# Linear attention: gates amid alternating query and key tiles, paired state updates; products behind layer norms; first scores amid value tiles

## The chip, the cores and the metric

The kernel runs on one core of one Trainium2 chip. The time is device microseconds of that core. The kernel before took 1971.51 us (median of three runs, 1969.75 to 1971.76). A change of under about 0.2% (3.9 us) can't be told from none.

## The reference, cut to what matters

Two blocks for 512 tokens of width 1024, all in float32. The first: a hybrid mixer, cross attention and a gated convolution layer. The second has two layers, each followed by a layer norm after its mixer and one after its MLP, so four in all:

```python
for i in range(2):
    mix = nsa_pool_mixer(x, ...) if i % 2 == 0 else gla_mixer(x, ...)
    x = layer_norm(ALPHA * x + mix, ln1_g[i], ln1_b[i])
    x = layer_norm(ALPHA * x + sqrelu_mlp(x, ...), ln2_g[i], ln2_b[i])
```

The NSA mixer is attention over compressed, selected and window keys for 8 query heads in 2 groups, beside a pooling path. The linear-attention mixer (GLA) has 4 heads with keys of 128 and values of 256 features. It projects x to queries, keys, values, a gate of rank 16 and an output gate r. The log gates are a log-sigmoid of the rank-16 gate times a second weight; they are summed within each chunk of 64 tokens. Per chunk the output is the masked local scores times the values, plus the query times the state left by the chunks before it; the state decays and takes in the chunk's keys times values. The output is normed and multiplied by silu(r).

## The kernel before, in words

Activations lie in SBUF with features on the partitions (8 chunks of 128) and 512 tokens along the free axis. A weight matrix is a stream of tiles of 128 x 1024 floats: SyncE loads each into one of four slots, GpSimd splits it into a high and a low part in fp32r (L2334 and L2336), and TensorE makes three fp32r products of 128x512 per chunk (high by high, high by low, low by high), 24 for a whole tile. A tile ends with `tile_done`; GpSimd may refill its slot then. VectorE or ScalarE takes the result out of the PSUM bank and counts `tile_out`; `claim` (in `dense`) makes TensorE wait for the `tile_out` of four tiles before. Each engine follows an order written out by hand, and waits on semaphores hold up all that is queued behind them.

**Layer norms.** `residual_ln` on VectorE adds each of the 8 result tiles into h (`take`, L1736), and keeps a running sum over chunks (L1698, for the last one L1700). TensorE turns it into the mean in all partitions by a product with ones (`sum_features`, L563), and the squares likewise (`sum_squares`, L556). Mean and squares give the variance (VectorE L1709), ScalarE the inverse root (L1164, L1165), and then, per chunk, VectorE scales (L1718), ScalarE writes the high part (L1237) and VectorE the low part (L1725). The next stage begins with `opening_of`: three tiles at once, chunk by chunk, six products for the high part of a chunk (L493, L494), three for its low part (L497).

**NSA.** Two tiles give the values by tokens (`tokens`, products of 128x256, L518 to L520) after the last key tile. Then come the scores of the first batch (`n_scores(0)`, L895 and L899), turns of the compressed probabilities (L942), the scores of batch 1, which reuse the banks of the values and so wait for them to be taken out (ScalarE L1475), and a pipeline over 16 batches: maximum on VectorE (L2153), exponentials on ScalarE (`n_exp`, L1462), scaling, turns and value products.

**GLA.** Nine tiles (gate, four of queries, four of keys), then four products of 16x512 for the gates' second weight (L1021), then two groups of four value tiles (`tokens`, 128x512, L518 to L520). ScalarE takes out all queries and keys and then works through the gates head by head in turns with VectorE: bias, Abs, Exp, Ln (L1531 to L1534), scan on VectorE (L2236, L2237), two exponentials, three products on VectorE (L2239, L2240, L2242), an exponential (L1541), a product (L2246, counts `gla_k`). The value tiles are taken out after heads 1 and 3 (L1160). `gla_scores` (L1048, turns L1052) waits for all four heads. Then eight tiles of r (`r_tile`, L1033 to L1035); among the chunks of the first four lie seven state updates each (`gla_updates`, L1066), one after each chunk from the second on. VectorE makes the states (L2266, L2269), and the next update but one waits for a state because the updates alternate between two banks. `gla_out` makes, for each block of 128 tokens, a local product (L1084) and one or two state products (L1088).

Of the kernel before, what the change touches and what calls it, by code (L numbers as in the profile page):

```python
# [25 lines left out]
S = 512  # L26
MEM = 256
KC = D // P
# [90 lines left out]
def chunk(c):  # L119
    return slice(c * P, (c + 1) * P)  # L120


def weight_stream(i):
# [5 lines left out]
    def add(w, cols, k0=0, kc=KC):  # L129
        tiles.append(tile_of(w, k0, kc, cols))  # L130
# [54 lines left out]

    mlp(0)
    add(c_in, slice(3072, 3088))
    for c in range(8):
        add(c_in, chunk(c))
    for half in range(2):  # L190
        add_wide(c_in[:, D + half * 512:D + (half + 1) * 512], 512)
    for c in range(KC):
# [259 lines left out]
def tensor_program(pr, pe):  # L452
# [45 lines left out]
                if k == kc - 1:  # L498
                    last.then_inc(sem("tile_done"), 1)

    def tokens(t0, width, hi, lo, blocks):

        per = TILE // width
        tiles = KC // per
        for j in range(tiles):
            pe.wait_ge(sem("weights_split"), t0 + j + 1)
            w_hi, w_lo = (m[w][:, (t0 + j) % RING].rearrange("p k n -> p (k n)") for w in ("w_hi", "w_lo"))
            for b in range(blocks):  # L510
                per_bank = 512 // width
                first, final = b % per_bank == 0, b % per_bank == per_bank - 1
                if j == 0 and first:
                    pe.wait_ge(sem("tile_out"), t0 + b // per_bank - RING + 1)
                out = acc[:, (t0 + b // per_bank) % RING, blk(b % per_bank, width)]
                for i in range(per):
                    k = j * per + i
                    mm(out, hi[:, k, blk(b)], w_hi[:, blk(i, width)], start=k == 0 and first, stop=False)  # L518
                    mm(out, hi[:, k, blk(b)], w_lo[:, blk(i, width)], start=False, stop=False)  # L519
                    last = mm(out, lo[:, k, blk(b)], w_hi[:, blk(i, width)], start=False,  # L520
                              stop=k == KC - 1 and final)
            last.then_inc(sem("tile_done"), 1)

    def late_opening(t0, first_tile, norm):

# [32 lines left out]
    def sum_features(name, part):  # L558


        i = LAYER_NORMS.index(name)
        pe.wait_ge(sem("ln_sum"), 2 * i + part + 1)
        mm(misc[:, 0, :], ones, m["sum_h"], start=True, stop=True).then_inc(sem("ln_mean"), 1)  # L563


    pe.wait_ge(sem("const_in"), 16)
    def idle_products(n):

        for _ in range(n):
            mm(acc[:, 0], ones, m["const"][:, 0:S], start=True, stop=True)  # L570

    idle_products(2)
    sum_squares("mix")
# [308 lines left out]

    pe.wait_ge(sem("cmp_gap"), 2)
    pool_out(0)
    tokens(t0 + 13, 256, x_hi, x_lo, TB)

    def n_scores(b):

# [44 lines left out]
                          start=False, stop=b == last_of(tb) and sb == tb)  # L933
        last.then_inc(sem("n_values"), 1)

    pe.wait_ge(sem("tile_out"), t0 + 13)
    n_scores(0)
    pe.wait_ge(sem("n_const"), 1)
    for half in range(2):
        pe.wait_ge(sem("cmp_p"), half + 1)  # L940
# [43 lines left out]
    def normed_stage(name, norm):  # L984

        for c in range(3, KC):
            if c == HALF + 1:
                sum_features(norm, 0)
            dense(START[name] + c, (START[name] + c) % RING, y_hi, y_lo)
        sum_features(norm, 1)  # L990
        sum_squares(norm)

    def mlp_group(name, g, norm, high, next_norm=None):
        t0 = g * 16 + START[name]
        opening(t0, START[name], norm)
        for j in range(3, 8):
            dense(t0 + j, (START[name] + j) % RING, x_hi, x_lo)
        opening_of(t0 + 8, START[name] + 8, y_hi, y_lo, high, "tile_out", g * 8, ready_before=t0)
        for c in range(3, KC):
            if next_norm and c == HALF + 1:  # L1000
                sum_features(next_norm, 0)
            dense(t0 + 8 + c, (START[name] + 8 + c) % RING, y_hi, y_lo)
        if next_norm:
            sum_features(next_norm, 1)
            sum_squares(next_norm)

    def mlp(name, norm, high, next_norm):
        with pe.Fori(0, GROUPS - 1) as g:
# [5 lines left out]
    mlp("mlp_a", "ln1a", "mlp_a_high", "ln2a")  # L1014


    stage("gla_in", x_hi, x_lo, 9, norm="ln2a")
    gate_w2 = pr.view("gate_w2").rearrange("p (h n) -> p h n", h=4)
    pe.wait_ge(sem("tile_out"), START["gla_in"] + 1)
    for head in range(4):  # L1020
        mm(misc[:, head, :], gate_w2[0:16, head], m["a_g"][0:16], start=True, stop=True).then_inc(sem("gla_z"), 1)  # L1021
    for part in range(2):
        tokens(START["gla_in"] + 9 + 4 * part, 512, x_hi, x_lo, TB)

    def r_tile(c, beside=None):

# [28 lines left out]
    def gla_updates(head):  # L1055

        def beside(k):
            if k == 0:
                return
            n = k - 1  # L1060
            i = 7 * head + n
            if n == 0:
                pe.wait_ge(sem("gla_kd"), head + 1)
            if i >= 2:
                pe.wait_ge(sem("gla_state"), i - 1)
            mm(misc[:, 1 + i % 2, 0:256], m["kd_tok"][blk(n % 2, 64), head % 2, n // 2],  # L1066
               m["v_g"][blk(n % 2, 64), n // 2, blk(head, 256)], start=True, stop=True).then_inc(sem("gla_update"), 1)
        return beside

    def o_bank(head, tb):  # L1070
# [4 lines left out]
    def gla_out(head):  # L1075
# [29 lines left out]
    def feature_beside(head, e, step):  # L1105
# [40 lines left out]
def scalar_program(pr, act):  # L1146
# [322 lines left out]
            .then_inc(sem("n_y_high"), 1)  # L1469

    pool_high(0)
    act.wait_ge(sem("tile_out"), t0 + 13)
    act.wait_ge(sem("tile_done"), t0 + 15)
    for tb in range(TB):
# [7 lines left out]
    n_exp(0)  # L1482
    n_exp(1)
    pool_high(1)
    for b in range(len(BATCHES)):
# [33 lines left out]

    t0 = START["gla_in"]  # L1520
    out(t0, t0 % RING, m["a_g"][0:16], src=acc[0:16, t0 % RING])
    for c in range(4):
        out(t0 + 1 + c, (t0 + 1 + c) % RING, m["q_g"][:, c])
    for c in range(4):
        out(t0 + 5 + c, (t0 + 5 + c) % RING, m["k_g"][:, c])
    gz, gt, gb = m["gz"], m["gt"], m["gb"]
    for head in range(4):
        act.wait_ge(sem("gla_z"), head + 1)
        if head:
            act.wait_ge(sem("gla_k"), head)  # L1530
# [1 line left out]
        own.link(f(gt, gz, ACT.Abs))  # L1532
        own.link(f(gt, gt, ACT.Exp, scale=-1.0))
        f(gt, gt, ACT.Ln, bias=1.0).then_inc(sem("gla_ln"), 1)  # L1534
        act.wait_ge(sem("gla_b"), head + 1)
        f(gz, gb, ACT.Exp, scale=1.0 / 16).then_inc(sem("gla_exp"), 1)
        f(gt, gb, ACT.Exp, scale=-1.0 / 16).then_inc(sem("gla_exp"), 1)
# [4 lines left out]
        if head % 2:  # L1542
            t = t0 + 9 + 4 * (head // 2)
            for b in range(TB):
                out_wide(t + b, t + 3, m["v_g"][:, b, blk(head // 2, 512)])
    def gla_kd(head):
        act.wait_ge(sem("gla_turned"), head + 1)
        if head >= 2:
# [48 lines left out]
def vector_program(pr, dve):  # L1597
# [74 lines left out]
    def residual_ln(name, t0, add):  # L1672
# [751 lines left out]
```

## Time and profile before

| | us |
|---|---|
| median of the runs | 1971.51 |
| profiled execution, its own time | 1971.24 |
| its span, first to last instruction | 1969.4 |
| TensorE busy | 1897.1 (96%) |
| GpSimd busy | 1069.4 (54%) |
| VectorE busy | 791.0 (40%) |
| ScalarE busy | 432.1 (22%) |
| mean granted TensorE clock | 0.987 of full |

The profile's page gives busy times and the chain of work that ended last. TensorE's idle time is what the rest of the span consists of, and it lies in few places; the timeline of one engine in a window shows each piece, with the engine and line that ended it in brackets. A product that shows 0.39 us starts 0.23 us after the one before it: the records overlap, so costs are read from start to start. The products of a 32-bit operand that isn't fp32r have two records each (x2 is one product).

### The profile page before, as it was taken

The page shows a single profiled execution, that of the slowest core. Times are in us where ns is not written, and L with a number is a line of the kernel's source. Part 1 is how long each engine was busy: PE and PEld are TensorE (multiplying, and loading weights), DVE is VectorE, ACT ScalarE, POOL GpSimd, SP SyncE. Part 2 cuts the span into 40 slices and gives each one's busy share as a digit, 9 for nine tenths or more (in the row PEclk, how much of TensorE's full clock was granted, in tenths as well). Part 3 has the DMA queues.
Part 4 walks back from the last instruction along what each step waited for, and adds up shares of the span by engine and source line. Part 5 has one row for each costly group of instructions (what it writes and reads, how often), then busy time and mean ns, then how long its engine had stood idle before and what let it go on. Part 6 is the DMA issues. An engine that isn't in the chain of part 4 may idle for free.

```text
span 1969.4 us, 24294 instructions
## 1 busy us (share of the span) xinstructions
PE 1897.1 (96%) x8906; PEld 1517.2 (77%) x8906; DVE 791.0 (40%) x1309; ACT 432.1 (22%) x850; POOL 1069.4 (54%) x622
## 2 busy tenths in 40 slices
PE   7989999999999999999999999998999989999996
PEld 5868787888888888866778888887765768888885
DVE  4965333352432435678451212135243372112126
ACT  4323422310000121155140101113323141101022
POOL 4735662566758666410546556664642446666652
PEclk9989999999999999999999999999999999999999
DMA  5322331232323335210223223332321223333321
GB/s 217 107 65 75 98 106 54 86 97 96 108 86 117 97 96 199 67 37 1 75 80 101 87 85 96 104 100 74 97 65 33 65 70 102 107 99 103 96 86 43
DMA packets 46880, 175.99 MB, mean 89 GB/s; under 512 B 5201, under 2 KB 5329, under 8 KB 46033
## 3 DMA queue, kind: packets, MB, share of 16 engines
q1 hardware_dynamic: 46512, 169.55, 27.1%
q10 hardware_dynamic: 288, 5.31, 0.7%
q8 instruction: 59, 0.97, 0.2%
q14 instruction: 21, 0.16, 0.0%
HBM read 172.74 MB, written 2.10 MB: 89 GB/s over the span
## 4 chain that ended last, share of the span: by engine, by line
PE 93%; DVE 4%; ACT 2%; issue 1%; DMA 0%; SPq 0%; DVEq 0%; ACTq 0%
PE acc L470 17%; PE acc L472 17%; PE acc L471 17%; PE acc L493 7%; PE acc L494 7%; PE acc L497 7%; PE acc L1033 1%; PE misc L1066 1%; PE acc L518 1%; PE misc L911 1%; PE acc L519 1%; PE acc L520 1%; PE acc L1035 1%; PE acc L1034 1%; PE acc L534 1%; PE acc L535 1%
## 5 line engine op out<-in xcount | busy, mean ns | idle before, releaser
L2334 POOL TENSOR_SCALAR w_hi<-raw 128x1024 fp32r<-128x1024 f32 x309 | 330.0, 1068 | 842.2 <-PE acc L497 329.5
L2336 POOL TENSOR_TENSOR w_lo<-raw,w_hi 128x1024 fp32r<-128x1024 f32 x309 | 744.1, 2408 | 25.8
L470 PE MATMUL acc<-x_hi,w_hi 128*128 128x512 f32 x872 | 342.8, 393 | 0.0
L472 PE MATMUL acc<-x_hi,w_lo 128*128 128x512 f32 x872 | 339.6, 389 | 0.0
L471 PE MATMUL acc<-x_lo,w_hi 128*128 128x512 f32 x872 | 339.3, 389 | 0.0
L470 PE MATMUL acc<-y_hi,w_hi 128*128 128x512 f32 x590 | 231.1, 392 | 0.0
L1736 DVE TENSOR_TENSOR h<-acc,h 128x512 f32<-128x512 f32 x120 | 82.9, 691 | 367.4 <-PE acc L472 233.8
L472 PE MATMUL acc<-y_hi,w_lo 128*128 128x512 f32 x590 | 229.6, 389 | 0.0
L471 PE MATMUL acc<-y_lo,w_hi 128*128 128x512 f32 x590 | 229.6, 389 | 0.0
L472 PEld LDWEIGHTS acc<-x_hi,w_lo 128*128 128x128 f32 x872 | 163.7, 188 | 34.4
L471 PEld LDWEIGHTS acc<-x_lo,w_hi 128*128 128x128 f32 x872 | 163.9, 188 | 32.5
L470 PEld LDWEIGHTS acc<-x_hi,w_hi 128*128 128x128 f32 x872 | 163.8, 188 | 32.4
L1508 ACT ACTIVATE z<-acc 128x512 f32<-128x512 f32 x64 | 38.2, 597 | 466.1 <-PE acc L497 354.9
L493 PE MATMUL acc<-y_hi,w_hi 128*128 128x512 f32 x330 | 130.0, 394 | 4.2 <-ACT y_hi L1368 2.9
L2211 DVE TENSOR_TENSOR acc<-acc,z 128x512 f32<-128x512 f32 x64 | 44.6, 697 | 216.1 <-ACT z L1508 216.1
L471 PEld LDWEIGHTS acc<-y_lo,w_hi 128*128 128x128 f32 x590 | 110.8, 188 | 23.9 <-issue 1.0
L494 PE MATMUL acc<-y_hi,w_lo 128*128 128x512 f32 x330 | 129.1, 391 | 0.0
L470 PEld LDWEIGHTS acc<-y_hi,w_hi 128*128 128x128 f32 x590 | 110.7, 188 | 23.9 <-issue 1.0
L472 PEld LDWEIGHTS acc<-y_hi,w_lo 128*128 128x128 f32 x590 | 110.7, 188 | 23.1
L493 PE MATMUL acc<-x_hi,w_hi 128*128 128x512 f32 x240 | 97.1, 404 | 15.3 <-ACT x_hi L1237 12.2
L494 PE MATMUL acc<-x_hi,w_lo 128*128 128x512 f32 x240 | 96.5, 402 | 0.0
L497 PE MATMUL acc<-y_lo,w_hi 128*128 128x512 f32 x330 | 93.1, 390 | 1.4 <-DVE y_lo L2317 1.4
(387 smaller groups left out, 2648.2 us busy)
## 6 DMA issues: line engine op xcount, KB each, us to landing
raw<-weights_dram SPq DMA_DIRECT2D x309, 512.0 KB, 3.6
w_cmp<-w_cmp_dram ACTq DMA_DIRECT2D x1, 4096.0 KB, 14.6
h<-x_dram SPq DMA_DIRECT2D x2, 1024.0 KB, 6.4
out_dram<-h SPq DMA_DIRECT2D x8, 256.0 KB, 2.0
small<-small_dram SPq DMA_DIRECT2D x1, 1408.0 KB, 16.0
small<-small_dram ACTq DMA_DIRECT2D x1, 1088.0 KB, 5.0
mem_in<-mem_dram SPq DMA_DIRECT2D x1, 1024.0 KB, 13.2
const<-const_dram SPq DMA_DIRECT2D x1, 640.0 KB, 9.3
```

The costliest lines, as they stand in the source:

```text
L470: mm(out, m["w_hi"][:, slot, k], hi[:, k], start=k == 0, stop=False)
L471: mm(out, m["w_hi"][:, slot, k], lo[:, k], start=False, stop=False)
L472: last = mm(out, m["w_lo"][:, slot, k], hi[:, k], start=False, stop=k == kc - 1)
L493: mm(acc[:, slot], m["w_hi"][:, slot, k], hi[:, k], start=k == 0, stop=False)
L494: mm(acc[:, slot], m["w_lo"][:, slot, k], hi[:, k], start=False, stop=False)
L497: last = mm(acc[:, slot], m["w_hi"][:, slot, k], lo[:, k], start=False, stop=k == kc - 1)
L518: mm(out, hi[:, k, blk(b)], w_hi[:, blk(i, width)], start=k == 0 and first, stop=False)
L1508: f(z[:, slot], acc[:, slot], ACT.Relu).then_inc(sem(name + "_relu"), 1)
L1736: v.tensor_tensor(h[:, c], acc[:, slot], h[:, c], ALU.add).then_inc(sem("tile_out"), 1)
L2211: v.tensor_tensor(acc[:, slot], acc[:, slot], z[:, slot], ALU.mult).then_inc(sem(name + "_product"), 1)
L2334: nc.gpsimd.tensor_scalar(hi, m["raw"][:, slot], 1.0, 0.0, ALU.mult, ALU.add).then_inc(sem("weights_high"), 1)
L2336: nc.gpsimd.tensor_tensor(m["w_lo"][:, slot].rearrange("p k n -> p (k n)"), m["raw"][:, slot], bf(hi), ALU.subtract).then_inc(sem("weights ...
```

## The change

- The stream alternates the query and key tiles of GLA. After the gate, query 0, key 0 and query 1 tiles come four times one gate product (L1021) and one whole tile, then the last key tile. ScalarE takes tiles out between the heads' gates; `gla_gate` is the part up to Ln, `gla_exps` the rest.
- The value tiles count a semaphore `gla_v` after each block of the last tile, so that the first three banks are taken out (`v_out`) before the tile ends. `gla_scores(0)` moves from behind the second group of value tiles to between the two groups.
- State updates come in pairs: 0 and 1 after the second chunk, 2 and 3 after the fourth, 4 and 5 after the sixth, 6 after the eighth.
- `gla_out` makes its four local products first and the state products after them.
- The second mean of a layer norm is two products that accumulate: the sum without the last chunk, then the last chunk itself once its tile is out. VectorE's last addition goes. After the sum of squares TensorE makes four products of ones (128x512, 32-bit), whose result isn't used, into the bank of the next stage's first tile; not after the last layer norm.
- `n_scores(0)` moves between the two value tiles of NSA, and `n_exp(0)` on ScalarE ahead of the values' taking out.

```diff
-    for c in range(8):
+    for c in range(4):
         add(c_in, chunk(c))
+        add(c_in, chunk(4 + c))
@@ tokens
+                if ready and j == tiles - 1 and b < blocks - 1:
+                    last.then_inc(sem(ready), 1)
             last.then_inc(sem("tile_done"), 1)
+            if beside:
+                beside(j)
@@ sum_features, part 1 (part 0 as before)
+        mm(misc[:, 0, :], ones, m["sum_h"], start=True, stop=False)
+        first = N_TILES if name == LAYER_NORMS[-1] else START[BEFORE_STAGE[name]]
+        pe.wait_ge(sem("tile_out"), first)
+        mm(misc[:, 0, :], ones, m["h"][:, KC - 1], start=False, stop=True).then_inc(sem("ln_mean"), 1)
+        sum_squares(name)
+        if first < N_TILES:
+            idle_products(4, first % RING)
@@ NSA, TensorE
-    tokens(t0 + 13, 256, x_hi, x_lo, TB)
...
-    pe.wait_ge(sem("tile_out"), t0 + 13)
-    n_scores(0)
+    def first_scores(j):
+        if j == 0:
+            pe.wait_ge(sem("tile_out"), t0 + 13)
+            n_scores(0)
+
+    tokens(t0 + 13, 256, x_hi, x_lo, TB, beside=first_scores)
@@ GLA, TensorE
-    stage("gla_in", x_hi, x_lo, 9, norm="ln2a")
+    stage("gla_in", x_hi, x_lo, 4, norm="ln2a")
...
     for head in range(4):
         mm(misc[:, head, :], gate_w2[0:16, head], m["a_g"][0:16], start=True, stop=True).then_inc(sem("gla_z"), 1)
-    for part in range(2):
-        tokens(START["gla_in"] + 9 + 4 * part, 512, x_hi, x_lo, TB)
+        t = START["gla_in"] + 4 + head
+        dense(t, t % RING, x_hi, x_lo)
+    dense(START["gla_in"] + 8, START["gla_in"] % RING, x_hi, x_lo)
@@ gla_updates
-            if k == 0:
+            if k % 2 == 0:
                 return
...
+            for n in range(k - 1, min(k + 1, 7)):
+                i = 7 * head + n
+                if i >= 2:
+                    pe.wait_ge(sem("gla_state"), i - 1)
+                mm(...)
@@ gla_out
         for tb in range(TB):
+            mm(o_bank(head, tb), m["att_g"][:, head % 2, tb], m["v_g"][:, tb, blk(head, 256)], start=tb % 2 == 0, stop=False)
+        for tb in range(TB):
             out = o_bank(head, tb)
-            mm(out, m["att_g"][:, head % 2, tb], m["v_g"][:, tb, blk(head, 256)], start=tb % 2 == 0, stop=False)
@@ GLA, TensorE
+    tokens(START["gla_in"] + 9, 512, x_hi, x_lo, TB, "gla_v")
     gla_scores(0)
+    tokens(START["gla_in"] + 13, 512, x_hi, x_lo, TB, "gla_v")
@@ GLA, ScalarE
+    q_out(0); k_out(0); q_out(1)
+    gla_gate(0); gla_exps(0); k_out(1); q_out(2)
+    gla_gate(1); gla_exps(1); k_out(2); q_out(3)
+    gla_gate(2); k_out(3); gla_exps(2)
+    gla_gate(3); gla_exps(3)
+    v_out(0)
...
     gla_kd(0)
+    v_out(1)
     r_out(0)
@@ residual_ln, VectorE
-            if k < KC - 1:
+            if k < KC - 2:
                 own.link(v.tensor_tensor(part, part, h[:, k], ALU.add))
-            else:
+            elif k < KC - 1:
                 v.tensor_tensor(total, part, h[:, k], ALU.add).then_inc(sem("ln_sum"), 1)
```

(The ScalarE calls stand one to a line in the kernel; `n_exp(0)` moves in the same way from behind the values' taking out to ahead of it.)

## Rows read from the trace of the kernel before

**Rows 1.** The page, chain of work that ended last, shares by engine.

```profile
PE 93%; DVE 4%; ACT 2%; issue 1%; DMA 0%; SPq 0%; DVEq 0%; ACTq 0%
```

**Rows 2.** Timeline, TensorE, third of four layer-norm ends: start us, us, what.

```profile
1340.42 1.12 PE L563 MATMUL misc<-sum_h,const 128*128 128x512 f32 x2 [1.58 <-DVE sum_h L1700]
1341.38 1.02 PE L556 MATMUL misc<-sum_sq,const 128*128 128x512 f32 x2
1346.45 0.77 PE L493 MATMUL acc<-x_hi,w_hi 128*128 128x512 f32 x1 [4.05 <-ACT x_hi L1237]
...
1349.97 0.40 PE L493 MATMUL acc<-x_hi,w_hi 128*128 128x512 f32 x1
```

**Rows 3.** Timelines of VectorE and ScalarE, the same stretch.

```profile
1338.94 0.69 DVE L1736 TENSOR_TENSOR h<-acc,h 128x512 f32<-128x512 f32 x1 [2.04 <-PE acc L472]
...
1340.33 0.69 DVE L1619 TENSOR_TENSOR sum_sq<-misc,sq 128x512 f32<-128x512 f32 x1
1342.44 0.70 DVE L1709 SCALAR_TENSOR_TENSOR misc<-misc,sq 128x512 f32<-128x512 f32 x1 [1.41 <-PE misc L556]
...
1347.35 0.74 DVE L1725 SCALAR_TENSOR_TENSOR x_lo<-misc,par,x_hi 128x512 fp32r<-128x512 f32 x1
...
1345.62 0.69 ACT L1237 ACTIVATE x_hi<-misc,par 128x512 fp32r<-128x512 f32 x1 [1.25 <-DVE misc L1718]
```

**Rows 4.** Timeline, TensorE, products of ones at the kernel's start.

```profile
15.81 1.88 PE L570 MATMUL acc<-const 128*128 128x512 f32 x4
```

**Rows 5.** Windows: us, busy us (x) of each engine; PEclk is the granted clock.

```profile
1346.40:1350.00 3.60, 3.55 (x10) 2.87 (x11) 3.60 (x7) 2.04 (x3) 0.00 (x0) 0.58 0.00 0
1400.00:1404.00 4.00, 4.00 (x10) 2.71 (x9) 1.92 (x2) 1.95 (x5) 0.74 (x1) 0.58 0.36 131
```

**Rows 6.** Timeline, TensorE, gate products, second group of value tiles, first scores.

```profile
1398.81 1.88 PE L1021 MATMUL misc<-a_g,small 16*128 16x512 f32 x4
...
1425.04 0.47 PE L518 MATMUL acc<-w_hi,x_hi 128*128 128x512 f32 x1 [0.78 <-ACT v_g L1160]
...
1449.45 0.69 PE L1048 MATMUL misc<-q_g,kt_g 128*64 128x64 f32 x16 [2.37 <-DVE k_g L2246]
```

**Rows 7.** Timelines of ScalarE, VectorE, GpSimd in the gates.

```profile
1398.15 0.69 ACT L1531 ACTIVATE gz<-misc,par 128x512 f32<-128x512 f32 x1 [0.46 <-PE misc L1021]
...
1407.53 0.69 ACT L1531 ACTIVATE gz<-misc,par 128x512 f32<-128x512 f32 x1 [0.82 <-DVE k_g L2246]
...
1432.14 2.92 DVE L2239 TENSOR_TENSOR kt_g<-k_g,gt 128x512 f32<-128x512 f32 x1 [1.22 <-ACT gt L1537]
...
1432.11 2.39 POOL L2336 TENSOR_TENSOR w_lo<-raw,w_hi 128x1024 fp32r<-128x1024 f32 x1
```

**Rows 8.** Timeline, TensorE, updates among r tile 0, products of head 0.

```profile
1455.06 0.70 PE L1066 MATMUL misc<-v_g,kd_tok 64*128 64x256 f32 x2
...
1456.58 0.70 PE L1066 MATMUL misc<-v_g,kd_tok 64*128 64x256 f32 x2
...
1475.32 0.70 PE L1084 MATMUL acc<-v_g,att_g 128*128 128x256 f32 x2
1475.94 0.65 PE L1088 MATMUL acc<-state,q_g 128*64 128x256 f32 x4
```

**Rows 9.** Timeline, TensorE, scores in NSA.

```profile
848.16 1.16 PE L895 MATMUL acc<-k_br,q_n 64*128 64x128 f32 x16
...
849.72 1.04 PE L942 MATMUL misc<-const,e_c 128*128 128x128 f32 x8
...
856.91 1.13 PE L895 MATMUL acc<-k_br,q_n 64*128 64x256 f32 x8
```

**Rows 10.** Timelines of VectorE and ScalarE, the same stretch.

```profile
840.46 0.68 DVE L1745 TENSOR_TENSOR k_br<-acc,r_late 128x512 f32<-128x512 f32 x1
...
848.33 1.57 ACT L1475 ACTIVATE v_br<-acc,r_col 128x256 f32<-128x256 f32 x4 [10.88 <-PE acc L520]
...
853.93 0.40 ACT L1462 ACTIVATE p_n<-acc,n_neg 128x128 f32<-128x128 f32 x1
```

More of the change, by code:

```diff
@@ L499, in opening_of, with tokens @@
                     last.then_inc(sem("tile_done"), 1)
-    def tokens(t0, width, hi, lo, blocks):
+    def tokens(t0, width, hi, lo, blocks, ready=None, beside=None):
         per = TILE // width
@@ L562, in sum_features, with idle_products @@
         pe.wait_ge(sem("ln_sum"), 2 * i + part + 1)
-        mm(misc[:, 0, :], ones, m["sum_h"], start=True, stop=True).then_inc(sem("ln_mean"), 1)
+        if part == 0:
+            mm(misc[:, 0, :], ones, m["sum_h"], start=True, stop=True).then_inc(sem("ln_mean"), 1)
+            return
+        mm(misc[:, 0, :], ones, m["sum_h"], start=True, stop=False)
[5 more added lines that the diff above has]
+            idle_products(4, first % RING)
     pe.wait_ge(sem("const_in"), 16)
-    def idle_products(n):
+    def idle_products(n, slot=0):
         for _ in range(n):
-            mm(acc[:, 0], ones, m["const"][:, 0:S], start=True, stop=True)
+            mm(acc[:, slot], ones, m["const"][:, 0:S], start=True, stop=True)
     idle_products(2)
@@ L990, in normed_stage @@
         sum_features(norm, 1)
-        sum_squares(norm)
     def mlp_group(name, g, norm, high, next_norm=None):
@@ L1004, in mlp_group @@
             sum_features(next_norm, 1)
-            sum_squares(next_norm)
     def mlp(name, norm, high, next_norm):
@@ L1057, in beside @@
         def beside(k):
-            if k == 0:
+            if k % 2 == 0:
                 return
-            n = k - 1
-            i = 7 * head + n
-            if n == 0:
+            if k == 1:
                 pe.wait_ge(sem("gla_kd"), head + 1)
[L1064 to L1067, printed above, removed]
+            for n in range(k - 1, min(k + 1, 7)):
+                i = 7 * head + n
+                if i >= 2:
+                    pe.wait_ge(sem("gla_state"), i - 1)
+                mm(misc[:, 1 + i % 2, 0:256], m["kd_tok"][blk(n % 2, 64), head % 2, n // 2],
+                   m["v_g"][blk(n % 2, 64), n // 2, blk(head, 256)], start=True, stop=True).then_inc(sem("gla_update"), 1)
         return beside
@@ L1471, in scalar_program @@
     pool_high(0)
+    n_exp(0)
     act.wait_ge(sem("tile_out"), t0 + 13)
@@ L1481, in scalar_program @@
     f(m["pct"][:, 0:4], misc[:, 1, :].rearrange("p (j n) -> p j n", j=4), ACT.Copy).then_inc(sem("cmp_pt"), 1)
-    n_exp(0)
     n_exp(1)
@@ L1521, in scalar_program, with q_out, k_out, gla_gate @@
     out(t0, t0 % RING, m["a_g"][0:16], src=acc[0:16, t0 % RING])
[L1522 to L1525, printed above, removed]
+    def q_out(c):
+        out(t0 + 1 + 2 * c, (t0 + 1 + 2 * c) % RING, m["q_g"][:, c])
+    def k_out(c):
+        out(t0 + 2 + 2 * c, (t0 + 2 + 2 * c) % RING, m["k_g"][:, c])
     gz, gt, gb = m["gz"], m["gt"], m["gb"]
-    for head in range(4):
+    def gla_gate(head):
         act.wait_ge(sem("gla_z"), head + 1)
@@ L1534, in scalar_program, with gla_exps @@
         f(gt, gt, ACT.Ln, bias=1.0).then_inc(sem("gla_ln"), 1)
+    def gla_exps(head):
         act.wait_ge(sem("gla_b"), head + 1)
@@ L1541, in scalar_program, with v_out @@
         f(gz, gz, ACT.Exp, scale=1.0 / 16).then_inc(sem("gla_exp"), 1)
[L1542 to L1545, printed above, removed]
+    def v_out(part):
+        t = t0 + 9 + 4 * part
+        for b in range(TB):
+            if b < TB - 1:
+                act.wait_ge(sem("gla_v"), (TB - 1) * part + b + 1)
+                f(m["v_g"][:, b, blk(part, 512)], acc[:, (t + b) % RING], ACT.Copy).then_inc(sem("tile_out"), 1)
+            else:
+                out_wide(t + b, t + 3, m["v_g"][:, b, blk(part, 512)])
+    q_out(0)
+    k_out(0)
+    q_out(1)
+    gla_gate(0)
+    gla_exps(0)
+    k_out(1)
+    q_out(2)
+    gla_gate(1)
+    gla_exps(1)
+    k_out(2)
+    q_out(3)
+    gla_gate(2)
+    k_out(3)
+    gla_exps(2)
+    gla_gate(3)
+    gla_exps(3)
+    v_out(0)
     def gla_kd(head):
```

## The prediction

> **What bounds the kernel now.** I read the chain of waits first: 93% of what ended last is TensorE [rows 1]. Dense fp32r products are untouched by this change, so I went on to TensorE's timeline and looked for its gaps, for stretches at the lower clock, and for places where products of another kind cost more than their columns. The second group of value tiles is 96 products from 1425.04 to 1447.08 (the next gap's start, 1449.45 less 2.37), 0.228 us each [rows 6]; a whole tile of 24 is 5.46. Each layer norm but the last leaves TensorE idle for 1.58 and then 4.05 us [rows 2], and the products after it run at a granted clock of 0.58 [rows 5]. GLA has gaps of 0.78 and 2.37 us [rows 6], a second stretch at 0.58 [rows 5], and a state update that lengthens each chunk of an r tile from 0.68 (three products) to 1.52 [rows 8].
>
> **Layer norms (four ends, three followed by an opening).** Take the one at 1338.94; the others read alike. VectorE's addition ends at 1339.63, its sum takes until 1340.4, the mean product starts at 1340.42, the squares' product behind it at 1341.38, and L1709 at 1342.44 [rows 2, 3]. After the change the first mean product runs while VectorE adds the last chunk (its input is ready a tile earlier), and the second starts at about 1339.70 and lets go at 1340.66 (0.96 start to start [rows 2]). The squares' sum on VectorE runs from 1340.33 to 1341.02 as before [rows 3], so their product starts at 1341.09 in place of 1341.38: the chain gains 0.3, not the 0.7 of the addition removed, because the squares are late next. This holds at all four ends.
>
> The four products of ones: two took 1.88 at full clock, 0.94 each [rows 4]. Started at 1341.09 + 0.96 = 1342.05 they end at 1345.8. The opening's first operand comes at 1346.45 - 0.3 = 1346.15, so they end 0.35 before it is wanted and cost nothing. What they change is the clock. Before, the opening's first chunk took from 1346.45 to 1349.97, 3.52 us for nine products [rows 2], at 0.58 [rows 5]. The idle time before it was 4.05, and 1.58 a little earlier; now no gap there is over 0.5, so I take the full level of 2.4 GHz: six products from 1346.15 to 1347.5, then a wait for the low part (its end, 1348.09, less 0.3 = 1347.8 [rows 3]), three products to 1348.5. The second chunk starts 1.45 earlier. From there TensorE's own 2.05 per chunk is slower than the 1.9 of VectorE and ScalarE, so the gain stays. 3 x 1.45 + 0.3 = 4.6 us. If the clock falls in spite of them, 4 x 0.3 = 1.2 stays. The Trainium skill (TensorE: Matmul & The Clock Gate, Part 1) says that an idle engine falls to the lower clock and busy work lifts it again; the trace agrees, at 0.58 after the 4.05 us.
>
> **GLA: gates amid the tiles.** TensorE's work up to r tile 0 stays: 6 dense tiles after the opening, 4 gate products, 192 products of value tiles, scores and turns 1.03. What goes is: the clock after four gate products in a row of 16 rows each (0.58 from 1400 to 1404 [rows 5]: its nine products cost 3.5 for 2.05, so 1.45; a single such product between whole tiles gives no such stretch, I take it); the gap of 0.78 and its restart, 0.95, since three of four banks are now taken out while the tile runs; the gap of 2.37, 2.5 with its restart, if the gates are done in time [rows 6]. With 0.3 of pipeline ends this is 5.2. Bounds: 3.7 if the clock falls again, 5.2 above, as nothing else idles there.
>
> Are the gates in time? A head's chain takes 9.38 us without GpSimd (1398.15 to 1407.53 [rows 7]). GpSimd's split of a tile holds up VectorE products of two SBUF operands: L2239 at 1432.14 took 2.92 in place of 0.69, while L2336 ran from 1432.11 [rows 7]; a hit costs up to 2.2. I put GpSimd's splits (1.07 + 2.39, started by the tile that frees the slot) beside the new order. With all of it 1.4 earlier: gate 0 starts at 1369.3, head 0 is hit three times and ends at 1382.4; gate 1 starts at 1382.8 and ends at 1394.2; gate 2 starts at 1394.7 (behind the query tile of 1393.6), waits for the last key tile at 1399.0, ends at 1406.0; gate 3 ends at 1417.0. The scores want it at the end of the first value group: the opening's end (1349.97 + 7 x 2.04 = 1364.26, now 1362.8) + 6 x 5.45 + 4 x 0.88 + 21.85 = 1420.9. 3.9 us are spare, so the chain is hidden. The tiles held up behind it on ScalarE: key 1 leaves its bank at 1382, and the first that needs that is the last key tile at 1393.6; key 2 at 1394 against 1400.4; key 3 at 1399.7 against 1403.2. None waits. The first value bank is ready at 1416.9, when ScalarE is just free. `gla_scores(0)` needs no bank of the values. r tile 0 then starts 5.2 + 1.45 earlier.
>
> **Paired updates.** Before, an update costs 1.52 - 0.68 = 0.84, though its 256 columns in a 32-bit operand are about 0.43 by the 0.94 of 512 [rows 8, 4]: half is for going from one kind of product to the other and back. Of a pair the second goes without that: 0.43 more. And the two use different halves of the rows (64*128) and different banks; four such products of 256 in NSA (x8, two records each, alternating halves) take 1.13 in all, 0.28 each (at 856.91 [rows 9]). A pair then costs between 0.84 (second free) and 1.46 (0.84 + the 0.62 of an isolated L1084 [rows 8]); I take 1.05, nearest to the NSA row. An r tile saves 3 x (1.68 - 1.05) = 1.9, for the tiles of heads 0 to 2 5.6 us (bounds 2.0 and 7.6). The added wait: the second update of a pair wants the state of the one two before, which VectorE now makes in a run of two (0.43 to 0.48 each, done about 1.05 after the pair); the next pair comes 1.37 after it, so 0.3 is spare. In head 3 it isn't: VectorE has a gain and a scaling (0.75 and 1.65) among the states, update 3 waits about 0.4 and updates 4 and 5 another 0.6. I give that tile 0.9. Sum 6.5.
>
> The skill (TensorEngine Tiling (Array Packing), Key Properties) says that a change of tiling mode drains the engine and that different row tiles run in parallel. Both would be in the 0.84 and in the 0.28 that the rows show. By its factor of up to 2 a pair would be at the lower bound, 0.84, and the kernel 1.9 us faster than I say.
>
> **`gla_out`.** Now a block of 128 tokens costs 0.62 for the local product (1475.32 to 1475.94) and 0.59 for two state products (0.65 less the overlap with what follows) [rows 8]. In a run the local ones should cost 0.43 + 0.06 = 0.49 and a pair of state products about 0.5 (a little under the NSA row's 0.28 each). That is 3 x 0.13 + 3 x 0.09 = 0.65 per head; I take 0.6, 2.3 us for four heads; bounds 0 and 3.4 (columns alone). The first blocks now finish later, but ScalarE's two squares for them (0.7) still fit before the last block's.
>
> **NSA.** The value tiles end at 848.16 [rows 9]; the second's 48 products of half the columns take half of 0.228 and a little more each, 5.8, so the first ends at about 842.3. The last key tile's output ends at 841.14 [rows 10], so `n_scores(0)` doesn't wait. It takes 1.56 (848.16 to 849.72 [rows 9]) and pushes the end of the value tiles and the values' taking out (1.57 on ScalarE, 848.33 to 849.90 [rows 10]) by as much, to 851.45. The scores of batch 1 need that bank: they started at 850.69, behind the turns (0.97 after 849.72); now 851.5, 0.8 later. Their maximum then ends at 854.5. `n_exp(0)` is done by 848, but before, `n_exp(1)` started at 853.93 [rows 10], right behind it and 0.3 after its own maximum. So the exponentials that were the bound are replaced by the later scores: 0.6 us later, and the chain `n_exp(1)`, pool output, maximum 2, `n_exp(2)` passes it on. Cost 0.6 (bounds -1.0, if the lighter ScalarE catches up later, and 1.6, the whole scores).
>
> **Sum.** 4.6 + 5.2 + 6.5 + 2.3 - 0.6 = 18.0 us off the profiled execution's own 1971.24: 1953.2. Its span was 1.84 shorter. The median of the runs is 0.27 above that execution, so 1953.5.
>
> **Rivals.**
> A. The products of ones don't hold the clock. For it: the fall after the gate products came although TensorE was busy all through them. Against: the second pair of products of ones at the start ran at 0.94 each, the full level. LN gain 1.2 in place of 4.6: 1956.9. 10%.
> B. Pairs cost what two updates cost alone: 1.46, and the waits for states bite. For it: the rows show the two halves side by side only without waits between. The r tiles give 2.0 + 0.3 and `gla_out` 1: 1959. 17%.
> C. The gate chain isn't done by 1420.9. Two more hits by GpSimd use up the 3.9 spare; two beyond that cost 2 to 4: 1957. 10%.
> D. The other side: the gate chain becomes the bound of the whole stage. ScalarE holds query and key tiles behind it, so that value tiles stall on their banks. From 1369.3 to 1420.9 each head has 12.9 us; the chain eats the whole gain at (51.6 + 18.0)/4 = 17.4 us per head, and at 18.5 the kernel is slower by 4.4: 1976. Measured without GpSimd 9.38, worst with it 13.1. It would need every one of the five VectorE products of a head to be hit (9.38 + 5 x 2.2 = 20.4). 2%.
> E. The edits do little together (the clock in both places falls, the pairs at 1.46, no gain in `gla_out`): 18.0 - 3.4 - 1.5 - 4.3 - 2.3 = 6.5, 1965. 4%.
>
> **Chances.** The forecast 57%, A 10, B 17, C 10, D 2, E 4. Range 1949.5 (pairs at 0.84, `gla_out` at its upper bound, and NSA a little better) to 1960.5, which takes in A, B and C and leaves out E and D. About 0.2% (3.9 us) is what can be told from no change. Faster 0.95, within 0.03, slower 0.02.
>
> **What would show it.** Layer norms: the opening's first products 0.23 apart and the second chunk 1.45 earlier; L1709 0.3 earlier against L1736. GLA: no gap between gate products and value tiles, none before `gla_scores`, granted clock 1.0 throughout, and 81.0 us from the end of the opening to r tile 0 in place of 86.2 (1364.26 to 1450.48). r tiles 0 to 2: 9.4 in place of 11.3. `gla_out`: 4.1 in place of 4.7. NSA: `n_exp(1)` 0.6 later. Wrong if r tiles stay over 10.5, if VectorE's states lag behind the pairs, or if TensorE waits for `gla_k` between the value groups.

## The result, and the profile after

The changed kernel took 1950.07 us (median of 4 runs, 1948.35 to 1950.29), the kernel before 1970.97 beside it on the same chip (4 runs, 1969.75 to 1971.76). The ratio is 0.989, with a 95% interval of 0.9878 to 0.9903: about 21 us faster, where I had forecast 18.0. The profiled execution took 1950.14 us, its span was 1948.4 and the mean granted clock 0.991 of full (0.987 before). Every part of the change gained or lost in the direction that I had worked out. Three terms had the wrong size, and one had the right size for a wrong reason.

Chain of work that ended last, from the page of the changed kernel [rows 1]:

```profile
PE 94%; DVE 3%; ACT 1%; issue 1%; DMA 0%; SPq 0%; DVEq 0%; ACTq 0%
```

TensorE's timeline at the same layer-norm end as in rows 2 (it is the second of the four, not the third as they call it: TensorE's full means start at 982, 1340, 1594 and 1953 in the kernel before); L570 and L573 are the two parts of the mean, L560 the squares, L583 the products of ones:

```profile
1338.15 1.02 PE L570 MATMUL misc<-sum_h,const 128*128 128x512 f32 x2
1339.16 1.12 PE L573 MATMUL misc<-h,const 128*128 128x512 f32 x2
1340.60 1.13 PE L560 MATMUL misc<-sum_sq,const 128*128 128x512 f32 x2 [0.32 <-DVE sum_sq L1669]
1341.57 3.60 PE L583 MATMUL acc<-const 128*128 128x512 f32 x8
1345.78 0.47 PE L494 MATMUL acc<-x_hi,w_hi 128*128 128x512 f32 x1 [0.62 <-ACT x_hi L1255]
...
1347.47 0.97 PE L498 MATMUL acc<-x_lo,w_hi 128*128 128x512 f32 x3
1348.28 0.39 PE L494 MATMUL acc<-x_hi,w_hi 128*128 128x512 f32 x1
```

VectorE there [rows 3]:

```profile
1338.41 0.69 DVE L1786 TENSOR_TENSOR h<-acc,h 128x512 f32<-128x512 f32 x1 [2.12 <-PE acc L473]
1339.86 0.69 DVE L1669 TENSOR_TENSOR sum_sq<-misc,sq 128x512 f32<-128x512 f32 x1 [0.75 <-ACT sq L1190]
1341.77 0.70 DVE L1759 SCALAR_TENSOR_TENSOR misc<-misc,sq 128x512 f32<-128x512 f32 x1 [1.22 <-PE misc L560]
```

The two idle stretches of 1.58 and 4.05 us have become 0.32 and 0.62. The opening's first six products are 0.23 apart (0.31 behind the first), and the second chunk begins 2.50 after the first (3.52 before). The windows answer to [rows 5]; the third column from the right is the granted clock:

```profile
1346.00:1350.00 4.00, 3.93 (x17) 2.90 (x17) 4.00 (x8) 2.67 (x4) 0.00 (x0) 1.00 0.00 0
1369.00:1373.00 4.00, 4.00 (x18) 3.20 (x18) 1.02 (x1) 2.58 (x4) 3.92 (x4) 1.00 0.45 138
```

TensorE in GLA [rows 6]: a gate product (L1035) ahead of a key tile, then the first scores and turns between the two groups of value tiles, and r tile 0, which now starts with no gap anywhere before it:

```profile
1368.10 1.12 PE L1035 MATMUL misc<-a_g,small 16*128 16x512 f32 x2
1369.15 0.50 PE L471 MATMUL acc<-x_hi,w_hi 128*128 128x512 f32 x1
...
1422.16 0.69 PE L1063 MATMUL misc<-q_g,kt_g 128*64 128x64 f32 x16
...
1445.06 0.39 PE L1048 MATMUL acc<-x_hi,w_hi 128*128 128x512 f32 x1
```

The gate chain ended on VectorE 3.0 us before those scores [rows 7]:

```profile
1418.37 0.75 DVE L2296 TENSOR_TENSOR k_g<-k_g,gz 128x512 f32<-128x512 f32 x1 [0.70 <-ACT gz L1566]
```

r tile 0 and the products of head 0 [rows 8]; L1081 x4 is a pair of updates, L1098 the local products, L1104 the state products:

```profile
1446.51 0.70 PE L1081 MATMUL misc<-v_g,kd_tok 64*128 64x256 f32 x4
1447.14 0.50 PE L1048 MATMUL acc<-x_hi,w_hi 128*128 128x512 f32 x1
...
1448.73 0.70 PE L1081 MATMUL misc<-v_g,kd_tok 64*128 64x256 f32 x4
...
1463.65 1.99 PE L1098 MATMUL acc<-v_g,att_g 128*128 128x256 f32 x8
1465.58 1.73 PE L1104 MATMUL acc<-state,q_g 128*64 128x256 f32 x13
```

Here is the surprise of the trace. A pair has the same record as a lone update, 0.70, and the next product starts 0.63 later in both cases.

NSA, TensorE [rows 9]:

```profile
851.86 1.16 PE L907 MATMUL acc<-k_br,q_n 64*128 64x128 f32 x16 [0.84 <-ACT v_br L1494]
...
862.77 1.97 PE L923 MATMUL misc<-const,p_n 128*128 128x128 f32 x8 [3.48 <-ACT pt_n L1511]
```

Stages of one trace are compared with the same stages of the other, since the work ahead of all edits shifted by itself from execution to execution (NSA's first pool product, which no edit reaches, started between 834.1 and 837.6 in the kernels below):

| stretch | before | after | gain | forecast |
|---|---|---|---|---|
| mean product of the 1st to that of the 2nd layer norm | 358.28 | 357.16 | 1.12 | 1.45 |
| 2nd layer norm, from VectorE's last addition into h to the opening's second chunk | 11.03 | 9.87 | 1.16 | 1.45 |
| 3rd layer norm to the mean product of the 4th | 359.46 | 357.18 | 2.28 | 1.45 |
| the last layer norm's end, from the same addition to the variance | 3.50 | 3.35 | 0.15 | 0.3 |
| GLA: end of the opening to r tile 0 | 86.2 | 82.5 | 3.7 | 5.2 |
| r tiles 0 to 3 (11.3, 11.3, 11.3, 11.7 before; 8.7, 8.8, 8.8, 10.2 after) | 45.7 | 36.6 | 9.1 | 6.5 |
| products of the four heads, `gla_out` (4.74 each before) | 19.0 | 14.8 | 4.2 | 2.3 |
| NSA: first pool product to the next stage's opening | 100.13 | 100.49 | -0.36 | -0.6 |

Less 0.2 by which the work ahead of the edits was longer, that is 21.1, against 21.0 by the spans (1969.4 to 1948.4).

### The profile page after: what moved, and what is told of

It reads as the page before. It is cut to its first block, busy times and chain, and to the rows that moved or that the text cites. A ratio compares the mean times of both kernels' runs of the same rounds, so it can differ in the third digit from the quotient of the medians.

```text
span 1948.4 us, 24354 instructions
## 1 busy us (share of the span) xinstructions
PE 1894.0 (97%) x8938; PEld 1517.1 (78%) x8938; DVE 791.6 (41%) x1305; ACT 432.0 (22%) x850; POOL 1071.2 (55%) x622
## 4 chain that ended last, share of the span: by engine, by line
PE 94%; DVE 3%; ACT 1%; issue 1%; DMA 0%; SPq 0%; DVEq 0%; ACTq 0%
PE acc L471 17%; PE acc L473 17%; PE acc L472 17%; PE acc L498 7%; PE acc L494 7%; PE acc L495 7%; PE acc L518 1%; PE acc L519 1%; PE acc L520 1%; PE acc L1048 1%; PE misc L923 1%; PE acc L1050 1%; PE acc L1049 1%; PE acc L539 1%; PE acc L538 1%; PE acc L537 1%
```

## The experiments

Eleven kernels were run, all cut from the changed kernel. Where no number of runs is given the kernel ran once, and what is said of it rests on its trace, stage by stage. Line numbers in their rows can differ from its by a few.

**1. `singles`: one update per chunk again, the rest as changed.**

```
 def beside(k):
-    if k % 2 == 0:
+    if k == 0:
...
-    for n in range(k - 1, min(k + 1, 7)):
+    for n in (k - 1,):
```

> The changed kernel with the state updates one per chunk again, from the second chunk on, all else as changed. Theory (the second update of a pair is free, 0.85 us for the pair against 0.84 for one alone): r tiles of heads 0 to 2 go from 8.8 us back to 11.3, that of head 3 from 10.2 to about 11.7, and the kernel is 9 us slower than the changed one, 1959. Rival (most of the shorter r tiles comes from the better clock or the earlier gates, not from the pairs): r tiles stay under 10 us and the kernel loses under 5 us.

Measured: 1959.19 (4 runs, 1957.77 to 1959.80; ratio to the kernel before 0.9931, 0.9914 to 0.9947). From r tile 0 to the last of the r tiles' dense work 88.35 us in place of 79.40: 8.95. TensorE in r tile 0:

```profile
1447.18 0.70 PE L1081 MATMUL misc<-v_g,kd_tok 64*128 64x256 f32 x2
1447.81 0.50 PE L1048 MATMUL acc<-x_hi,w_hi 128*128 128x512 f32 x1
```

One product or two, 0.63 from start to start: the second update of a pair is free, and the pairs are worth 9, not 6.5.

**2. `same_half`: both updates of a pair on the same 64 rows.** Half of the updates read the wrong tokens, so the states are not the reference's.

```
-mm(misc[:, 1 + i % 2, 0:256], m["kd_tok"][blk(n % 2, 64), head % 2, n // 2],
-   m["v_g"][blk(n % 2, 64), n // 2, blk(head, 256)], ...
+mm(misc[:, 1 + i % 2, 0:256], m["kd_tok"][blk(0, 64), head % 2, n // 2],
+   m["v_g"][blk(0, 64), n // 2, blk(head, 256)], ...
```

> The changed kernel with both updates of a pair reading rows 0 to 63 of keys and values, so half of the state updates are computed from the wrong tokens. Theory (the pair is cheap because its products use different row halves and run side by side): a pair costs 0.43 more, 1.28 in place of 0.85, r tiles 0 to 2 take 10.1 in place of 8.8 and the span grows by 5 us. Rival (the pair is cheap because the price of an update is nearly all the passage to another kind of product and back, shared by both): pairs stay at 0.85.

Measured: 1953.29, and 83.77 us for the r tiles in place of 79.40. TensorE in r tile 0:

```profile
1445.29 1.13 PE L1081 MATMUL misc<-v_g,kd_tok 64*128 64x256 f32 x4
1446.34 0.50 PE L1048 MATMUL acc<-x_hi,w_hi 128*128 128x512 f32 x1
```

From the pair's start to the next product there are 1.05, 0.42 more than in different halves, which is just the 256 columns; in the terms of the prediction the pair costs 1.27 in place of 0.85. So in the changed kernel the two halves of the array work side by side in full. The r tiles grew by 4.4 and not by the 5 expected: head 3's grew by 0.56 where the others grew by 1.27, since in two of its pairs the second update waits for a state already (see the account of the paired updates below).

**3. `locals_amid`: local and state products in turns again, the rest as changed.**

```
 for tb in range(TB):
-    mm(o_bank(head, tb), m["att_g"][:, head % 2, tb], ...)
-for tb in range(TB):
     out = o_bank(head, tb)
+    mm(out, m["att_g"][:, head % 2, tb], ...)
```

> The changed kernel with the local products of gla_out among the state products again. Theory (going between 128x128 and 128x64 products costs about 0.15 us each way): gla_out goes from 3.7 to 4.74 us for each head, the span is 4.2 us longer than the changed kernel's 1948.4. Rival (the 4.7 before came from waits for states, which are gone now): gla_out stays at 3.7.

Measured: 1952.67; the r tiles with their products took 83.56 in place of 79.40, so 4.16 for four heads. TensorE, head 0:

```profile
1462.01 0.70 PE L1099 MATMUL acc<-v_g,att_g 128*128 128x256 f32 x2
1462.64 0.65 PE L1103 MATMUL acc<-state,q_g 128*64 128x256 f32 x2
1463.22 0.70 PE L1099 MATMUL acc<-v_g,att_g 128*128 128x256 f32 x2
1463.85 0.65 PE L1103 MATMUL acc<-state,q_g 128*64 128x256 f32 x4
1464.43 0.70 PE L1099 MATMUL acc<-v_g,att_g 128*128 128x256 f32 x2
```

One state product (x2) and two (x4) both take 0.58 here. They differ in their 64 columns of the array, and they too run side by side.

**4. `gates_row`: the four gate products in a row again, the rest as changed.**

```
 for head in range(4):
     mm(misc[:, head, :], gate_w2[0:16, head], m["a_g"][0:16], ...)
+for head in range(4):
     t = START["gla_in"] + 4 + head
     dense(t, t % RING, x_hi, x_lo)
```

> The changed kernel with the four gate products in a row behind the query 1 tile and then the five tiles, ScalarE's order as changed. Theory (a gate product alone between fp32r tiles costs 1.27 us, in a row 0.91, because each passage is paid once): 4 x 0.36 = 1.4 us less from the opening to r tile 0, 81.1 in place of 82.5, if the granted clock stays at the full level behind them. Rival (four such products in a row bring the clock down again, as before the change): the next products run at 0.43 and 1.45 us are lost again, so 82.5 to 82.6.

Measured: 1949.38; from the opening's start to r tile 0 99.65 us in place of 99.28. TensorE, and then the window behind the four:

```profile
1366.96 3.69 PE L1035 MATMUL misc<-a_g,small 16*128 16x512 f32 x8
1370.58 0.50 PE L471 MATMUL acc<-x_hi,w_hi 128*128 128x512 f32 x1
...
1371.47 0.63 PE L471 MATMUL acc<-x_hi,w_hi 128*128 128x512 f32 x1
```

```profile
1370.50:1374.50 4.00, 4.00 (x12) 3.08 (x12) 3.45 (x2) 0.45 (x2) 3.92 (x3) 0.59 0.55 179
```

The clock fell again, right behind 3.6 us in which TensorE had no gap at all. What the row saves against single products is lost to the clock again, and 0.37 more. The kernel's own time, 0.7 under the changed kernel's median, does not contradict this: its NSA stage happened to be 0.96 shorter (point 7).

**5. `no_ones`: no products of ones behind the layer norms.**

```
 if first < N_TILES:
-    idle_products(4, first % RING)
+    idle_products(0, first % RING)
```

> The changed kernel without the four products of ones behind each layer norm; the mean in two products stays. Theory (the products only hold the clock): after three layer norms TensorE idles 4 us, the opening's first chunk runs at a granted clock of about 0.58 again and its second chunk starts 1.0 us later than in the changed kernel, more where the low stretch is long as it was after the third (2.1); in all 3 to 6 us more, 1953 to 1956. The variance comes at the same time after the last addition. Rival (the gain of the layer norms comes from the shorter chain): under 1 us.

Measured: 1954.19 (4 runs, 1952.36 to 1955.49; ratio 0.9907, 0.989 to 0.9923), 4.1 over the changed kernel by the medians and 5.3 by the spans of the two traces (the profiled execution was the longest of the four). Second layer norm:

```profile
1348.19 0.76 PE L494 MATMUL acc<-x_hi,w_hi 128*128 128x512 f32 x1 [4.05 <-ACT x_hi L1255]
1348.75 0.63 PE L495 MATMUL acc<-x_hi,w_lo 128*128 128x512 f32 x1
```

And a window of it:

```profile
1350.00:1352.00 2.00, 2.00 (x6) 1.58 (x5) 2.00 (x4) 1.44 (x3) 0.00 (x0) 0.50 0.00 0
```

The three stages behind an opening are 2.47, 1.89 and 1.03 longer than in the changed kernel. The gap is the same 4.05 each time; only the stretch of products at the lower level of 1.2 GHz differs, from 3.6 us in the shortest case (1585.54 to 1589.09) to over 6 in the longest (988.56 to about 995). This is what my working had overlooked.

**6. `eight_ones`: eight products of ones in place of four.**

```
-    idle_products(4, first % RING)
+    idle_products(8, first % RING)
```

> The changed kernel with eight products of ones in place of four. Theory (they fill 3.6 of the 4.2 us there, and what is over is paid on the path at 0.9 us each): the opening starts 3.0 us later, its second chunk 2.6 later, since it no longer waits for the first low part; three times, 7.7 us more span than the changed kernel's 1948.4, about 1956. Rival (TensorE catches up in the opening, whose chunks wait for VectorE anyway): under 3 us.

Measured: 1955.27. The stages behind the openings are 2.22, 2.21 and 2.22 longer than in the changed kernel, where I had expected 2.6 each; the work ahead of them was 1.5 shorter in this execution.

```profile
1342.27 7.03 PE L583 MATMUL acc<-const 128*128 128x512 f32 x16
1348.73 0.79 PE L494 MATMUL acc<-x_hi,w_hi 128*128 128x512 f32 x1
```

Products of ones are free only as long as they end before the first operand: four end at 1345.16 and the operand comes at 1345.78. These eight also held the full clock, 7 us of them, with nothing else running on TensorE.

**7. `nsa_back`: NSA's first scores behind all value tiles and their exponentials behind the turned operands, as before the change.**

```
-tokens(t0 + 13, 256, x_hi, x_lo, TB, beside=first_scores)
+tokens(t0 + 13, 256, x_hi, x_lo, TB)
+first_scores(0)
...
 pool_high(0)
-n_exp(0)
...
+n_exp(0)
 n_exp(1)
```

> The changed kernel with NSA's first scores behind both value tiles and their exponentials behind the values' taking out, as before. Theory (the move delays the scores of batch 1, which wait for the value banks): from the first pool product to the opening of the output stage 100.1 us in place of 100.5. Rival (the 0.4 is spread between executions): 100.4 to 100.6.

Measured: 1948.18. From the first pool product to the opening 98.74, where my figure was 100.1, and shorter than the kernel before with the same order. The trace splits it at the turns of the second batch (`n_turn(1)`), which follow the idle time of 3.48:

| kernel | pool product to `n_turn(1)` | `n_turn(1)` to `n_turn(2)` | `n_turn(1)` to the opening |
|---|---|---|---|
| before | 26.15 | 7.20 | 73.98 |
| changed | 26.84 | 6.91 | 73.65 |
| `gates_row`, changed order | 26.85 | 5.92 | 72.68 |
| `nsa_back` | 26.16 | 5.83 | 72.58 |

The first column is the same for one order in all kernels, to 0.03: moving the scores cost 0.69, near the 0.6 forecast. The second holds the stretch at the lower clock behind the gap, and it varies from 5.71 to 7.20 between kernels, and within one order of the work too: with the changed order six kernels show 6.9 to 7.0 and two 5.9. So the 0.36 that the stage lost is 0.69 of cause and 0.33 of this variation. The Trainium skill (TensorE: Matmul & The Clock Gate, Part 1) says that the same kernel can show different numbers of slow products at its start from run to run. The table shows the like behind a gap inside a kernel.

**8. `gates_two_nsa`: `nsa_back`, and two gate products ahead of every other tile.**

```
 for head in range(4):
+    if head % 2 == 0:
+        for h in (head, head + 1):
             mm(misc[:, h, :], gate_w2[0:16, h], m["a_g"][0:16], ...)
     t = START["gla_in"] + 4 + head
     dense(t, t % RING, x_hi, x_lo)
```

> The changed kernel with the gate products in twos (heads 0 and 1 behind the query 1 tile, 2 and 3 two tiles on), and NSA's order as before the change. Theory (a pair shares its passages and is too short to bring the clock down): from the opening to r tile 0 2 x 0.36 = 0.7 us less than the changed kernel's 82.5, NSA 0.4 less, so 1.1 in all, 1949.0. Rival (two in a row already bring the clock down, as four did): 1.4 us or more lost at one or both places, 1950.5.

Measured: 1947.78 (4 runs, 1947.08 to 1948.82; ratio 0.9876, 0.986 to 0.9893). The clock held, and the stage was 0.78 shorter up to the first pair of updates (99.95 in place of 100.73):

```profile
1367.58 1.98 PE L1038 MATMUL misc<-a_g,small 16*128 16x512 f32 x4
1369.49 0.50 PE L471 MATMUL acc<-x_hi,w_hi 128*128 128x512 f32 x1
```

The window behind the first pair:

```profile
1369.00:1371.00 2.00, 2.00 (x9) 1.25 (x8) 0.00 (x0) 1.90 (x4) 1.92 (x2) 1.00 0.45 98
```

From one gate product to the next there are 6.72 us in the changed kernel, 1.27 over a tile's 5.45. From pair to pair there are 13.02, 2.12 over two tiles. So the second product of a pair costs 0.85, and a pair saves 0.42 against two single ones. That is also the price of going over to this kind of product and back, once for each visit: 1.27 less 0.85, and the same 0.42 is left of 2.12 less twice 0.85.

**9 to 11. `after_again`, `two_again`, `nsa_ones`: the best version beside the changed kernel, on one chip.** The first two are the changed kernel and experiment 8 again. The third adds three products of ones into NSA's gap, in a bank that is free there:

```
 for b in range(len(BATCHES)):
+    if b == 1:
+        pe.wait_ge(sem("n_pool"), 2)
+        for _ in range(3):
+            mm(misc[:, 3], ones, m["const"][:, 0:S], start=True, stop=True)
     n_turn(b)
```

> The changed kernel once more, so that the two kernels below stand beside it on the same chip. From the first state-independent turn of NSA's second batch (behind the 3.48 us gap) to the opening of nsa_out the traces so far show two groups, 72.6 and 73.6 to 74.0, whatever the order of the work: a stretch at the lower clock of varying length. I expect one of the two again, and 1950 us.

> Gate products in pairs ahead of every other tile, and NSA's first scores behind the value tiles as before the change. Against the changed kernel my theory has 0.8 us from the gates (one passage between kinds of products saved per pair: 100.73 to 99.95 from the opening to the first update) and 0.69 from NSA (pool product 0 to the second batch's turns 26.84 to 26.15): 1948.5 by the median where the changed kernel has 1950.0. The rival: the 2.3 us between the medians so far were really gained, since the low stretch in NSA is shorter whenever the scores come late; then this kernel shows 72.6 again and the changed one 73.6 to 74.0.

> As two_again, and three products of ones into the free fourth bank before the turns of NSA's second batch, inside the gap of 3.48 us (0.9 each, from about 859.75 to 862.4, the turns at 863.3). Theory: the stretch at 0.5 that follows this gap goes, the turns take 1.03 and the scores 1.07, and the time from the turns to the opening falls from 72.6 (or 73.6 to 74.0) to about 71; 1.5 to 2.9 us faster than two_again by the trace. Rival: ScalarE's exponentials and VectorE's maxima bound this stretch, so the products at half speed were covered and nothing or under 0.3 us is gained; or the clock falls in spite of the three products.

| kernel | median (runs) | ratio to before, 95% | `n_turn(1)` to `n_turn(2)` | to the opening |
|---|---|---|---|---|
| `after_again` | 1949.48 (1948.55 to 1950.42) | 0.9880, 0.9864 to 0.9897 | 6.97 | 73.75 |
| `two_again` | 1947.16 (1945.68 to 1947.51) | 0.9871, 0.9854 to 0.9887 | 5.71 | 72.47 |
| `nsa_ones` | 1945.97 (1944.77 to 1947.86) | 0.9862, 0.9846 to 0.9878 | 4.30 | 71.41 |

NSA in `nsa_ones`, TensorE and then a window; L972 are the products of ones:

```profile
859.95 2.84 PE L972 MATMUL misc<-const 128*128 128x512 f32 x6
863.53 1.09 PE L923 MATMUL misc<-const,p_n 128*128 128x128 f32 x8 [0.74 <-ACT pt_n L1518]
864.55 1.13 PE L907 MATMUL acc<-k_br,q_n 64*128 64x256 f32 x8
```

```profile
864.00:866.00 2.00, 2.00 (x20) 1.35 (x19) 1.97 (x3) 1.21 (x5) 0.00 (x0) 1.00 0.03 8
```

And in `two_again`:

```profile
862.18 1.67 PE L907 MATMUL acc<-k_br,q_n 64*128 64x256 f32 x8
```

The stretch at the lower clock is gone, and the turns and scores take their full-speed 1.02 and 1.07. It gained 1.41 up to the next turns, of which 1.06 is left at the opening. That is under the 1.5 to 2.9 that I expected; `two_again` happened to have the shortest low stretch of all. Against the changed kernel's trace it is 2.34. By medians `nsa_ones` is 3.5 under the changed kernel with no overlap of their runs (4 each). Against `two_again` the runs overlap, so the 1.2 between those two rests on the traces. Whether late scores tend to shorten the low stretch stays open: with that order three kernels show 5.7 to 5.8 and the kernel before 7.2, and two with the other order show 5.9.

## Why the prediction was right and where it was wrong

**Direction and mechanism** stand in every part; sizes were off, and the time came out 3.4 us under the 1953.5 forecast, at the fast end of the range. Pairs brought 2.6 more than their term, `gla_out` 1.9 more and the gates 1.5 less, which is 3.0 of it. None of the rivals came about: the ones held the clock (against A), pairs cost the least possible (against B), the gate chain ended 3.0 us early, where I had 3.9 (against C and D), and the parts did much together (against E).

**Paired updates: the step that failed.** I put a pair at 1.05 between 0.84 and 1.46, "nearest to the NSA row" (0.28 each). It costs 0.85, the lower bound of 0.84. I had misread the NSA row: its 0.28 for each product holds the end of the run. The kernel before shows it in two runs of one pair of scores each, of 384 and of 512 columns:

```profile
880.77 0.92 PE L895 MATMUL acc<-k_br,q_n 64*128 64x384 f32 x4
899.58 1.13 PE L895 MATMUL acc<-k_br,q_n 64*128 64x512 f32 x4
```

The next products start at 881.62 and 900.65, so 128 columns more in both products of a pair cost 0.22, which is what they cost in one product (0.43 for 256). There too the two halves work side by side in full, and about 0.2 of each run is its end. The rule that I had weighed beside it, of the Trainium skill (TensorEngine Tiling (Array Packing), Key Properties), that different tiles can run in parallel, held here in full: `same_half` lengthens the pair by 0.42. I had written that the kernel would be 1.9 us faster by it; it was 2.6, since head 3's tile gained 1.5 in place of 0.9 as well, by the cheaper pairs alone. The waits in that tile were as I had charged them, 0.94 in place of 1.0; two of its pairs last 0.61 and 0.33 longer than 0.70 in the changed kernel, since their second updates wait for a state on VectorE (made at 1488.31 and 1490.86, the updates start at 1488.37 and 1490.91):

```profile
1487.75 1.31 PE L1081 MATMUL misc<-v_g,kd_tok 64*128 64x256 f32 x4
1490.58 1.03 PE L1081 MATMUL misc<-v_g,kd_tok 64*128 64x256 f32 x4
```

**`gla_out`: mis-sized, and its upper bound wrong.** I worked with three of four blocks per head. All four gain. And the state pair in a run costs 0.44 (1.75 for four), where I had 0.50; the local product costs 0.48, where I had 0.49. 4 x (0.14 + 0.14) is 1.1 per head, as `locals_amid` shows (4.16 for four); the upper bound of 3.4 carried the same count of three.

**Gates amid the tiles: too optimistic by 1.5.** All gaps went and the clock held. But I had priced a gate product at 0.88, from four in a row, though it now stood alone between tiles. It costs 1.27 there: 4 x 0.39 = 1.56, the whole miss. It is the price of going over and back (0.42) that I did count for the updates (0.84 less 0.43 of columns), and left out here. With 1.27 my own sum comes out as measured: 6 x 5.45 + 4 x 1.27 + 2 x 21.85 + 1.03 = 82.5. No kernel put the old order of the tiles or of their taking out back, so how the gain divides among these moves is not shown; that both gaps are gone is.

**Layer norms: 4.6 forecast and 4.7 measured, by errors that cancel.** The end of the norm gained 0.15, not 0.3: the squares' chain behind the last addition was unchanged in length to VectorE (1339.86 behind 1338.41 is 1.45, before 1.39), and its product now starts from idle and takes 0.1 longer. The stretch at full speed gained 0.97 and 1.02 at the first two openings, not 1.15. (A product of ones is 0.86 from start to start; my 0.94 was half of a record of two, which holds their end. So the four ended 0.62 before the operand and not 0.35, at no gain or loss.) The 0.3 missing in each of two openings and the 0.15 at the last end were made up by the third opening, which starts at 1600.03 and which I had called like the others. It was not. TensorE's timeline of the kernel before:

```profile
1604.01 0.63 PE L493 MATMUL acc<-x_hi,w_hi 128*128 128x512 f32 x1
...
1605.58 0.40 PE L493 MATMUL acc<-x_hi,w_hi 128*128 128x512 f32 x1
```

There the lower clock reached into the second chunk, which starts at 1604.01 (the idle time, which alone I had compared, was the same 4.05), and its removal gained 2.28. That the products of ones are worth 3 to 5 us as a whole is shown by `no_ones`: 4.1 by the medians, 3.3 by the two ratios to the kernel before, 5.3 by the traces.

**NSA: -0.6 forecast, -0.36 measured**, of which -0.69 is the mechanism, as forecast, and +0.33 the clock's variation.

## What to carry over

Cost a product by its neighbours: between products of another kind this kernel paid 0.3 to 0.4 us for going over and back, so the same product has one price in a row and another alone, and two small products in different halves of the array cost what one does, as long as neither waits. An idle gap of 3.5 or 4 us on TensorE cost twice here, itself and the low clock behind it, while gaps of 0.62 did not; the second part has no fixed length, so read it at each place and in more than one execution, and fill the gap with full-size products that end before the awaited operand. When two executions differ by a microsecond or two, compare stage by stage from fixed points before naming a cause.

## What was not expected of the hardware

- Four products of 16 rows in a row (3.6 us without a gap) were followed by a granted clock of 0.58 to 0.59, in the kernel before and in `gates_row`. Two in a row (1.98 us) were not, nor were eight products of ones on 128 rows (7.03 us).
- Two updates on different 64 rows: 0.63 from start to start, as one alone; on the same 64 rows 1.05. Two state products in different 64 columns: 0.58, as one alone.
- Behind the same gap of 4.05 us the low stretch lasted 3.6 to over 6 us; behind the gap of 3.48 us in NSA the time to the next turns was 5.71 to 7.20, and 4.30 with the gap filled.
